# Two layers with pooling and attention, then two mixer layers, on one core: another order of the pooling groups, and the last two tiles of each layer norm added before their sums

## The reference

```python
for i in range(DEPTH):
    h = _swiglu(x, ffn1_w_gate[i], ffn1_w_up[i], ffn1_w_down[i])
    x = _layer_norm(ALPHA * x + MACARON_WEIGHT * h, ln_gain[i, 0], ln_bias[i, 0])
    m = _pool_mixer(...) if i == 0 else _dilated_attention_mixer(...)
    x = _layer_norm(ALPHA * x + m, ln_gain[i, 1], ln_bias[i, 1])
    h = _swiglu(x, ffn2_w_gate[i], ffn2_w_up[i], ffn2_w_down[i])
    x = _layer_norm(ALPHA * x + MACARON_WEIGHT * h, ln_gain[i, 2], ln_bias[i, 2])
```

## Time and profile before

| what | value |
|---|---|
| median of 3 runs | 3483.22 us (3482.59 to 3483.66) |
| profiled execution | 3485.5 us |
| its span | 3483.7 us |
| mean granted TensorE clock | 0.995 of full speed |
| PE busy | 3421.0 us, 98% |
| POOL busy | 2521.6 us, 72% |
| DVE busy | 1503.3 us, 43% |
| ACT busy | 822.7 us, 24% |

### The profile page before, as it was taken

One profiled execution on the slowest core, in us unless ns is written; L12 is line 12 of the kernel. 1 busy time (PEld: TensorE's weight loads), 2 busy tenths in 40 slices (PEclk: granted clock), 3 DMA queues, 4 the chain that ended last, 5 costly groups with the idle time before them and its releaser, 6 DMA issues.

```text
span 3483.7 us, 48672 instructions
## 1 busy us (share of the span) xinstructions
PE 3421.0 (98%) x18708; PEld 2830.2 (81%) x18708; DVE 1503.3 (43%) x2307; ACT 822.7 (24%) x1463; POOL 2521.6 (72%) x2220
## 2 busy tenths in 40 slices
PE   9999989999999999999999999999999999999998
PEld 7887978888988888888888887877778787777876
DVE  5562562112311143344456114265656436565643
ACT  1110232110211022222234111122323222232322
POOL 9998787888788877665655888856566785655675
PEclk9999999999999999999999999999999999999999
DMA  6553222322233222122211332222222222222222
GB/s 220 189 182 102 83 85 85 96 93 92 93 96 95 89 93 88 63 72 73 73 62 49 108 96 94 85 82 67 62 72 67 85 85 85 64 61 76 64 82 73
DMA packets 322475, 312.08 MB, mean 90 GB/s; under 512 B 11616, under 2 KB 306176, under 8 KB 322048
## 3 DMA queue, kind: packets, MB, share of 16 engines
q1 hardware_dynamic: 304928, 277.91, 25.5%
q10 hardware_dynamic: 17376, 31.78, 2.8%
HBM read 307.56 MB, written 2.10 MB: 89 GB/s over the span
## 4 chain that ended last, share of the span: by engine, by line
PE 49%; issue 26%; POOL 21%; DVE 3%; ACT 1%; POOLq 0%; DMA 0%; DVEq 0%; SPq 0%
PE ps L1895 23%; POOL wh L349 14%; POOL wl L353 7%; PE ps L387 6%; PE ps L1566 4%; PE ps L598 3%; PE ps L1938 2%; PE ps L572 1%; PE ps L2471 1%; PE ps L1429 1%; PE ps L1475 1%; PE ps L2272 1%; PE ps L2243 1%; PE ps L905 1%; PE ps L1441 1%
## 5 line engine op out<-in xcount | busy, mean ns | idle before, releaser
L349 POOL TENSOR_TENSOR wh<-w_raw,zero 128x512 fp32r<-128x512 f32 (+3 forms) x1108 | 1156.0, 1054 | 931.4 <-PE ps L1895 379.1
L353 POOL TENSOR_TENSOR wl<-w_raw,wh 128x512 fp32r<-128x512 f32 (+3 forms) x1108 | 1423.0, 1295 | 0.0
L387 PE MATMUL ps<-xh,wh 128*128 128x512 f32 x1536 | 601.2, 391 | 2.7 <-POOL wl L353 1.5
L387 PE MATMUL ps<-xh,wl 128*128 128x512 f32 x1536 | 597.9, 389 | 0.0
L387 PE MATMUL ps<-xl,wh 128*128 128x512 f32 x1536 | 597.7, 389 | 0.0
L1895 PE MATMUL ps<-xh,wh 128*128 128x512 f32 x1072 | 444.0, 414 | 7.8 <-POOL wl L353 4.3
L1895 PE MATMUL ps<-xh,wl 128*128 128x512 f32 x1072 | 420.3, 392 | 0.0
L1895 PE MATMUL ps<-xl,wh 128*128 128x512 f32 x1072 | 420.2, 392 | 0.0
L387 PEld LDWEIGHTS ps<-xh,wh 128*128 128x128 f32 x1536 | 288.4, 188 | 65.5 <-POOL wl L353 3.4
L387 PEld LDWEIGHTS ps<-xl,wh 128*128 128x128 f32 x1536 | 288.4, 188 | 60.1 <-issue 1.0
L387 PEld LDWEIGHTS ps<-xh,wl 128*128 128x128 f32 x1536 | 288.3, 188 | 60.2
(11 more groups left out here) (372 smaller groups left out, 6046.9 us busy)
## 6 DMA issues: line engine op xcount, KB each, us to landing
w_raw<-in_w_in SPq DMA_DIRECT2D x120, 512.0 KB, 4.1
w_raw<-in_ffn_w_gate SPq DMA_DIRECT2D x88, 512.0 KB, 4.7
w_raw<-in_ffn_w_up SPq DMA_DIRECT2D x88, 512.0 KB, 4.8
w_raw<-in_attn_w_qkv SPq DMA_DIRECT2D x72, 512.0 KB, 4.5
w_raw<-in_ffn_w_down SPq DMA_DIRECT2D x64, 512.0 KB, 3.6
ada_raw<-in_ada_w ACTq DMA_DIRECT2D x24, 512.0 KB, 3.9
stats<-in_ada_w ACTq DMA_DIRECT2D x24, 512.0 KB, 4.1
w_raw<-in_ffn_w_down SPq DMA_DIRECT2D x32, 384.0 KB, 4.0
```

The source lines that it names most:

```text
L349: done.append(s["w_hi"].up(pool.tensor_tensor(hi[:, parts[q]], raw[:, parts[q]], zero, ALU.subtract)))
L353: s["w_lo"].up(pool.tensor_tensor(lo[:, parts[q]], raw[:, parts[q]], hi[:, parts[q]].bitcast(F32), ALU.subtract))
L387: mm = self.nc.tensor.matmul(out, a[:, slot, w], b(t), start=start and t == order[0] and q == 0, stop=stop and t == order[-1] and q == 2)
```

## The change

There are two edits. The first sets the order of the pooling groups to windows 4, 8, 16, 2 and lets the first product of `pe_out` take its eight input tiles in that same order. The weight columns of the projection are loaded in that order too, and the group matrices, which are one chunk, are used by quarters 1, 2, 3, 0.

```diff
-POOL_ORDER = (0, 1, 2, 3)
+POOL_ORDER = (1, 2, 3, 0)
@@ pe_out
-    self.product(..., before=before if n == 0 else None, order=range(done, KT))
+    self.product(..., before=before if n == 0 else None,
+                 order=first[done:] if n == 0 else range(done, KT))
@@ pe_pool
-                    before=lambda t: ...)
+                    before=lambda t: ..., first=POOL_TILES)
```

```diff
+    def pair_sum(self, what, h):
+        return self.half(self.squares[:, WHOLE + what], h)
@@ pe_half_sums(self, pe, st, h, parts=(0, 1))
-                    name = ("z_ready", "sq_ready")[what]
-                    pe.wait_ge(s[name].sem, st.at(name, WHOLE + 2 * h + n))
-                    part = self.tail_square(n - 1, h) if what else self.half(self.x[:, WHOLE + n - 1], h)
-                mm = self.nc.tensor.matmul(out, self.ones[:], part, start=n == 0, stop=n == 2)
+                    pe.wait_ge(s["tail_sums"].sem, st.at("tail_sums", 2 * h + what + 1))
+                    part = self.pair_sum(what, h)
+                mm = self.nc.tensor.matmul(out, self.ones[:], part, start=n == 0, stop=n == 1)
@@ pe_last
+        first, rest = ((0, 1), (2,)) if sums else ((0,), (1,))
...
-                        sums(pe, st, 0, (2,) if h else (0, 1))
+                        sums(pe, st, 0, rest if h else first)
@@ dve_norm
+        def tails(h):
+            tail(0, h)
+            tail(1, h)
+            for what in range(2):
+                name = ("z_ready", "sq_ready")[what]
+                dve.wait_ge(s[name].sem, st.at(name, WHOLE + 2 * h + 2))
+                parts = [self.tail_square(m, h) if what else self.half(self.x[:, WHOLE + m], h) for m in range(2)]
+                s["tail_sums"].up(nc.vector.tensor_tensor(self.pair_sum(what, h), *parts, ALU.add))
-        tail(0, 0)
-        tail(1, 0)
+        tails(0)
...
-                    tail(0, 1)
-                    tail(1, 1)
+                    tails(1)
```

More of the change, by code:

```diff
@@ L155 @@
 TAIL = KT + 2
-NORM = dict(zsum_ready=1, mean_ready=1, shifted=KT, tail_mm=2, sq_ready=TAIL, sums_ready=2, off_ready=2, off_squared=2, var_part=2, var_ready=2,
+NORM = dict(zsum_ready=1, mean_ready=1, shifted=KT, tail_mm=2, sq_ready=TAIL, sums_ready=2, tail_sums=4, off_ready=2, off_squared=2, var_part=2, var_ready=2,
             logs=2, std_ready=2, centred=2 * KT, t_ready=2 * KT, x_ready=KT, xh_ready=2 * KT, acts=2 * KT)
-POOL_ORDER = (0, 1, 2, 3)
+POOL_ORDER = (1, 2, 3, 0)
 POOL_TILES = tuple(2 * g + m for g in POOL_ORDER for m in range(2))
@@ L209 @@
 PRIMED = dict(acc=4, w_lo=8, gate_act=2, hid=2, hid_lo=2, z_ready=4)
-SIGNALS = ("acc w_hi w_lo gate_act hid hid_hi hid_lo z_ready zsum_ready mean_ready shifted tail_mm sums_ready off_ready off_squared var_ready logs centred sq_ready "
+SIGNALS = ("acc w_hi w_lo gate_act hid hid_hi hid_lo z_ready zsum_ready mean_ready shifted tail_mm sums_ready tail_sums off_ready off_squared var_ready logs centred sq_ready "
            "var_part std_ready t_ready x_ready xh_ready acts dve_step act_step "
@@ L519, in pe_shift, with pe_half_sums @@
         s["mean_ready"].up(self.nc.tensor.matmul(self.ps[:, self.shift_bank(st)], self.ones[:], self.zsum[:], start=True, stop=True))
-    def pe_half_sums(self, pe, st, h, parts=(0, 1, 2)):
+    def pair_sum(self, what, h):
+        return self.half(self.squares[:, WHOLE + what], h)
+    def pe_half_sums(self, pe, st, h, parts=(0, 1)):
         s = self.s
@@ L530, in pe_half_sums @@
                 else:
-                    name = ("z_ready", "sq_ready")[what]
-                    pe.wait_ge(s[name].sem, st.at(name, WHOLE + 2 * h + n))
-                    part = self.tail_square(n - 1, h) if what else self.half(self.x[:, WHOLE + n - 1], h)
-                mm = self.nc.tensor.matmul(out, self.ones[:], part, start=n == 0, stop=n == 2)
-            if n == 2:
+                    pe.wait_ge(s["tail_sums"].sem, st.at("tail_sums", 2 * h + what + 1))
+                    part = self.pair_sum(what, h)
+                mm = self.nc.tensor.matmul(out, self.ones[:], part, start=n == 0, stop=n == 1)
+            if n == 1:
                 s[signal].up(mm)
@@ L1202, in out_chunks, with pe_out @@
         return (2, [self.halves(w, 0, KT, (256 * mp, 512), 256) for mp in range(2)])
-    def pe_out(self, pe, st, c1, xs, before=None, residue=False, begun=0):
+    def pe_out(self, pe, st, c1, xs, before=None, residue=False, begun=0, first=tuple(range(KT))):
         for pair in range(3):
@@ L1213, in pe_out @@
                 done = begun if pair == 0 else 0
-                self.product(pe, (c1 + pair) % 2, KT, 256, m * P, self.ps[:, n % 4], xs, start=not done, before=before if n == 0 else None, order=range(done, KT))
+                self.product(pe, (c1 + pair) % 2, KT, 256, m * P, self.ps[:, n % 4], xs, start=not done, before=before if n == 0 else None,
+                             order=first[done:] if n == 0 else range(done, KT))
                 if n == 2:
@@ L1260, in pe_pool @@
         self.pe_out(pe, st, st.chunk0 + GROUPS + 1, ((lambda t: self.y_h[:, t]), (lambda t: self.y_l[:, t])),
-                    before=lambda t: pe.wait_ge(s["y_lo"].sem, st.at("y_lo", POOL_TILES.index(t) + 1)))
+                    before=lambda t: pe.wait_ge(s["y_lo"].sem, st.at("y_lo", POOL_TILES.index(t) + 1)), first=POOL_TILES)
     def act_pool(self, act, st):
```

## The result

The changed kernel takes 3490.85 us (median of 16 runs) against 3483.71 for the kernel before (16 runs beside it). The ratio is 1.0017, 95% interval 1.0010 to 1.0024: slower by 7.1 us. The bound named ahead, 0.2%, lies inside that interval; the slowdown itself is clear of zero. The forecast was 3491.7.

What follows compares the result with a forecast made beforehand. PE, 98% busy, with POOL's splitting of weights, was taken to bound the kernel. Norms +8.6, clock +3.0 and pooling -3.1 made +8.5 on 3485.5, less 2.3: 3491.7 us; likeliest 3489 to 3494, eight in ten 3477 to 3498.

Steps and rivals of the forecast that it cites:

- The sum: Whole kernel: norms +8.6, clock +3.0, pooling order -3.1 give +8.5 us against the profiled execution, 3491.7 us, 0.24% slower.
- Half 0 of the norms: Contended adds delay PE: +2.0 us over four feed-forward norms, +0.25 after pooling, -1.2 after attention, where POOL is done.
- +0.5 instead of -0.86: First norm, half 0: waits for two adds behind POOL make it cost +0.5 us instead of gaining 0.86.
- a bound of the clock: Lower bound of the clock term, -1.5 us: the fall after attention goes and none comes.
- Half 1: Adds delay low(1) and low(2): +1.0 us in each of three norms, +1.2 after pooling, +2.05 after attention, +1.3 in ffn 3.
- The clock: PE's waits ahead of tiles 1 and 2 bring two falls to half clock in five norms, 1.5 us each: +3.0.
- The pooling order: Pooling stage: the last group is ready sooner, but POOL's run of four chunks bounds the output product: -3.1 us.
- slow restart: Pooling stage: PE at 0.43 us per matmul after the 7.7 us wait, 463.87 to 466.5, counted inside the 3.3 gain.
- A: Rival: adds pass between POOL instructions without meeting them; half 0 -5.4, half 1 about 0, pooling -3.3: 3474.6 us; chance 0.12.
- B: Rival: norms lose but the clock holds, or the second add often follows directly: 3484 to 3488.7 us; chance 0.30.
- C: Rival: clock falls in nearly every norm (+7) and once in the pooling stage: +14, 3497.3 us; chance 0.13.
- D: Rival: pooling order gives nothing, as scale(1) or late group 3 holds the last group: +11.6, 3494.8 us; chance 0.05.

Runs made afterwards that it cites:

- e1: Kernel before with only the pooling order changed, norms as before: 3482.0 us, ratio 0.9990.
- e3: Full change, with one input of each add in PSUM (tile 6 evicted a second time, tile 7's square written there): 3480.66 us.
- f7: Full change, with pair sums in half 0 only, one add input in PSUM, half 1 back to six matmuls: 3473.25 us.
- e4: Full change, with each 128x256 add made in two 128x128 instructions, both inputs in SBUF: 3512.55 us.
- f5: Full change, with 11 dummy matmuls instead of 5 ahead of tile 1 in the first product after a norm: 3487.64 us.
- e2: Kernel before with only the norm sums changed, pooling order 2, 4, 8, 16 kept: 3493.87 us, ratio 1.0027.
- f8: f7 plus half 1 pair sums in five norms, one input in PSUM, adds behind low(2): 3472.04 us, ratio 0.9960.
- f6: Full change, with half 1's two adds moved on DVE behind low(2) in five norms, inputs still in SBUF: 3485.04 us.

## Why the prediction was right, step by step

**The sum.** Forecast +8.5 us against the profiled execution, measured +6.5 in the span and +7.1 in the medians. It stands on three terms; here is each with what it measured. The mechanism held. That the total came this near is in part luck: half 1 was put about 1.8 us too high, half 0 about 1.0 too low.

**Half 0 of the norms.** The step "+0.5 instead of -0.86" held almost to the hundredth: +0.50, +0.42, +0.50 and +0.49 in the four feed-forward norms, +0.19 after the pooling (forecast +0.25). The ends of the adds were forecast as 389.2 and 390.75 and came at 389.25 and 390.64. After attention it was -1.55, forecast -1.2, but for another reason than the forecast's. The forecast had POOL done when the adds come. It wasn't:

```profile
1879.36 0.45 DVE L793 TENSOR_TENSOR squares<-x 128x256 f32<-128x256 f32 x1
1879.81 1.41 DVE L793 TENSOR_TENSOR squares<-sq 128x256 f32<-128x256 f32 x1
```

```profile
1878.24 2.70 POOL L353 TENSOR_TENSOR wl<-w_raw,wh 128x512 fp32r<-128x512 f32 x2
```

The rows that I had read stood behind a fall of the clock, which held the tail of tile 7 back until POOL had ended. That fall is gone here, which I had left open as a bound of the clock, and with it the gap. e1, whose norms are those of before, has -1.54 at the same place without any pair sum. So the fall that is gone gave the whole -1.55, the adds gave nothing, and this step was right in its number by luck. With uncontended adds e3 and f7 have -3.08 there. Without that fall half 0 cost +2.1 in all, where the forecast had +1.05.

That two SBUF inputs are the reason is shown by e3 and e4 together: one takes the wait away and keeps the add, the other doubles the instructions and keeps the elements.

**Half 1.** Without a fall of the clock it cost, up to `variance` of half 1, 0.74 in ffn 0 and ffn 1 (f5) and 0.74 in ffn 2, forecast 1.0 each, and 0.96 after the pooling, forecast 1.2; up to the last low part 1.17, 1.18, 1.17 and 1.38, but that part doesn't last. After attention f5 has 1.71 (2.1 up to the last low part), forecast 2.05. For ffn 3 I gave +1.3; up to `variance` of half 1 the table has +0.89, and from `variance` of half 0 to the end -0.16. Between these points lies the whole second block, and with it falls of the clock that differ from one execution to the next. In f5, which has the same falls in the second block as before, the same stretch is 1.15 longer. So the loss is there, and in the changed kernel's own profile it is covered by a fall that the kernel before had and this one had not. The lasting costs add up to 5.8 us, where the forecast had 7.55.

**The clock.** Forecast two falls in five norms at 1.5 us, +3.0; there were three (ffn 0, ffn 1, attention) and f5 puts them at 1.3 to 1.6, 4.3 together. Against them stands the one that went after attention, 1.54: +2.8. This term is the least certain: it was a guess of a count, and it came near. The changed kernel and e2 have the same instructions up to the first norm and the same wait of 1.67 us there; the one has a fall behind it and the other has none.

**The pooling order.** Forecast -3.1, bounded by POOL's run of four chunks whose length was not to change. Measured -3.19 in e1 and -3.3 at the output product in the changed kernel; the run was 45.99 us against 45.96. The path inside was also as drawn: windows, scale(1) ahead of high(3), and a last group whose low part PE waits for, 1.7 us. No fall of the clock followed the waits of 1.4, 1.7 and less into which the wait of 7.7 us was cut. In the kernel before the clock went to its 1.2 GHz level within that wait, at 459.9, and came back at 466.7; that is the "slow restart" of the prediction:

```profile
463.40:466.80 3.40, 2.93 (x7) 2.38 (x8) 2.71 (x5) 0.90 (x2) 1.26 (x2) 0.51 0.20 55
```

**The rivals.** A (the adds don't meet POOL) is refuted for the change as it is, and e3 is the kernel in which its condition holds: half 0 then gained 1.03, I had given 0.76. But A put half 1 at about 0, and in e3 it loses 0.4 in the first norm up to `variance` of half 1 (0.8 up to the last low part); a second eviction stands there that A hadn't. f7 and f8 reach A's 3474.6 by leaving half 1 alone or moving its adds. B (the clock holds) is f5 without the dummy matmuls' own cost: 3487.64, in its range of 3484 to 3488.7. C and D didn't happen.

**What I would not claim.** That the 0.9 us per added instruction in e4 are all waits for POOL: its profile has nine stretches of 3.4 us at half clock in the norms, the changed kernel's has five (two of them in ffn 3), and they are in it too. That the count of falls was foreseen: e1 and e2 show that it changes where the code does not. And the 0.3 us by which POOL rather than DVE ends last in the pooling stage are too few to say what a faster POOL would bring; it wasn't tried.

## What to carry to other kernels

Before work moves from a full engine to an idle one, look at which inputs it reads and at who holds their path: here an add of 0.42 us took 0.59 and 1.46 us in the median because both inputs were in SBUF beside a busy POOL, and with one input in PSUM it took 0.42 again. Where such a piece goes in an in-order program counts too: behind the parts that the next engine waits for, the same adds of half 1 gave back 5.8 us, by the falls of the clock that stayed away and in two of the norms, though in the feed-forward norms without a fall the place made no gain. A row read behind a fall of the clock shows engines apart that meet when the fall is gone. An idle stretch may be limited by the next resource; the 7.7 us wait gave 3.3, since another engine had its own run of work up to there.

## What the runs showed of the hardware

- A DVE instruction with two SBUF inputs and POOL's take turns one by one. With the second add of a pair the wait was a whole POOL instruction: median 1.46 us against 0.42. In f6 the first add stands right behind a low part, which has two SBUF inputs too, and takes as long: 1.46 to 1.51 us in the three feed-forward norms where it stands there. That a row of such instructions pays each time, even at half the size (1.34 and 1.35 us for 128x128), was more regular than I expected.
- The granted clock went down (0.52 in the stretch behind) after a wait of PE of 1.67 us in the first norm, stayed up after one of 1.74 in ffn 2, the same place in the program, and in e2 stayed up after the same 1.67 in the first norm. Six more dummy matmuls ahead of tile 1, needed by nothing, removed the falls in the first five norms and 3.2 us. Such falls also make profiled executions differ where the code is the same: e1 is 5.3 us ahead of the kernel before at the last norm of the first block and 0.7 at the end. In the second block it runs at half clock for 10.2 us twice, where the kernel before has 6.8 and 3.4.
